# One-core two-block forward pass with a mixture of experts: the first two expert units' gates and ups put in a row, and down matrices loaded in two halves

## The chip, the cores and the metric

The program runs on one core of one Trainium2 chip. The metric is the device time of one execution in microseconds, from the first to the last work on the core. TensorE (PE) multiplies, VectorE (DVE) and ScalarE (ACT) work on tiles, GpSimd (POOL) issues the indirect DMAs, and SyncE (SP) issues nearly all weight loads, which 16 DMA engines carry.

## The reference

Float32 throughout, 512 tokens of width 1024. Block one: attention over a learned choice of keys, sliding-window attention, a dense MLP. Block two: gated linear attention and pooling, then the experts. Only the end of block two is touched:

```python
g_p, g_idx = lax.top_k(jax.nn.softmax(g_logits, axis=-1), 1)         # 1 of 4 groups
e_top, e_idx = lax.top_k(e_logits, TOP_K_IN_GROUP)                   # 2 of its 8 experts
gate = g_p * jax.nn.softmax(e_top, axis=-1)
def expert_block(args):                                              # D_EXPERT = 256
    xb, e = args
    return (jax.nn.silu(xb @ w_gate[e]) * (xb @ w_up[e])) @ w_down[e]
x = x + hier_moe(h2, ...)                                            # 32 experts, two per token
return rmsnorm_2(x, norm_f_g)
```

Gate, up and down of one expert are 1 MB each, so the experts need about 100 MB of weights.

## The kernel before, in words

The kernel runs five engines by hand with semaphores. Everything up to the residual stream of block two takes the first 1050 us and is not touched except for loads that start there. Then come 17 **units** (`UNITS_E`, q = 0 to 16). A unit is one or two experts of 64 rows each, stacked on 128 partitions; `places_of(q)` gives the numbers n of its experts' buffers in order of loading, `buffer_of(q)` the buffer of `xe` that holds its token rows.

Work of a unit, in the order of the data:

- POOL gathers its rows from `x_rows` in HBM into `xe` (line 691).
- PE turns them into `side` banks (`turn_rows_of`, line 2066), DVE copies them with the gain into `xeT` (`rows_turned`, line 1759).
- PE multiplies with gates and ups (`gate_up_part`, line 2408, 64 matmuls for two experts): the first 16 (`first_gates_of`, two parts of 8) run ahead, between the steps of the unit before, the other 48 in `gate_up_of`.
- ACT makes the silu (line 1159), DVE multiplies with the ups (`hidden`, line 1766), PE turns the result, ACT copies it, PE multiplies with the down matrices (`down_of`, line 2425, 16 matmuls).
- DVE adds to `xe` (`y_of`, line 1776). POOL scatters to `part_rows` (line 695). From unit 2 on (`FINISH_FROM`) the tokens that are then complete are normalised (`finish`, line 1787) and stored.

SP issues the loads in one order, each with a wait for the buffer's last reader: `gu` has 6 buffers (gates and ups of one expert, 2 MB, in four DMAs of 512 KB), `dn` has 8 (a down matrix, one DMA of 1 MB, `load_down`, line 548). SP's queue is in order: a wait holds back all loads behind it. Units 3 and 4 (`PIECED_E`) are loaded in quarters as units 0 and 1 release theirs (`gate_up_in_quarters`, line 613):

```python
for q in range(PIECED_E.start, EXTRA_AT + 1):
    for n in places_of(q):
        if n >= D_BUFS:
            sp.wait_ge(S("down_done"), unit_of(n - D_BUFS) + 1)
            down(n)
    if q in PIECED_E:
        gate_up_in_quarters(q)
        continue
```

Beside units 0 and 1, DVE also works out where the tokens go that an expert has beyond 64 rows: `late_columns` and `overflow_columns` (lines 1833 to 1864), `place_overflow` (1869 to 1881), `list_overflow` (1917 to 1921, after a small PE product, line 2478), and `name_late_experts` (1885 to 1908), whose last instruction raises `over_ready`. `gfin` is the final gain, broadcast to all partitions.

Of the kernel before, what the change touches and what calls it, by code (L numbers as in the profile page):

```python
# [13 lines left out]
P = 128  # L14
# [28 lines left out]
def buffer_of(q):  # L43

    return q if q < X_FIRST else (0, 1, 4, 5, 2, 3)[(q - X_FIRST) % X_BUFS]
# [202 lines left out]
def gated_blocks(nc, A, out):  # L248
# [8 lines left out]
    with stack:  # L257
# [107 lines left out]
        xe, _ = lay(b_at, ("xe", [P, X_BUFS, D]))  # L365
# [5 lines left out]
        assert temps_end <= b_at + 3 * half_buf  # L371
# [8 lines left out]
        below = place("below", [1, OVER, NE], b_at + words([P, X_FIRST + 1, D]))  # L380
        slotv = place("slotv", [P, 2, COLS], -(-tab_end // 64) * 64)
        gfin = place("gfin", [P, D], base + 4 * CONST_COLS["cos"][0])
# [67 lines left out]
        def _(sp):  # L450
# [151 lines left out]
            sp.dma_start(gfin[:, :], A["norm_f_g_2"].partition_broadcast(P)).then_inc(S("small_in"), 16)  # L602
# [62 lines left out]
        def _(pool):  # L665
# [24 lines left out]
            def gather(n, rows, done):  # L690
                pool.indirect_dma_start(xe[:, n, :], None, x_rows, bass.IndirectOffsetOnAxis(ap=rows, axis=0),
                                        bounds_check=row_bound, oob_is_err=False).then_inc(done, 16)

            def scatter(n, slots, done):
                pool.indirect_dma_start(part_rows, bass.IndirectOffsetOnAxis(ap=slots, axis=0), xe[:, n, :], None,
                                        bounds_check=row_bound, oob_is_err=False).then_inc(done, 16)

            def gather_parts(n, tokens, done):
                pool.indirect_dma_start(xe[:, n, :], None, part_rows, bass.IndirectOffsetOnAxis(ap=tokens, axis=0),
                                        bounds_check=row_bound, oob_is_err=False).then_inc(done, 16)  # L700

            def store_rows(n, tokens, done):
                pool.indirect_dma_start(out, bass.IndirectOffsetOnAxis(ap=tokens, axis=0), xe[:, n, :], None,
# [25 lines left out]
            for q in range(X_FIRST):  # L729
                gather(q, tabi[:, 1, q:q + 1], S(f"gathered{q}"))  # L730
            pool.wait_ge(S("slots_ready"), 1)
            pool.wait_ge(S("y_zeroed"), 16 * NT)
            for q in range(LAST_E):
# [7 lines left out]
                if q in (LAST_E - 3, LAST_E - 1):  # L741
                    pool.drain()
# [3 lines left out]
                if n < UNITS_E:  # L746
                    if q < 2:
                        scattered(q)
                    if q == 2:
                        pool.wait_ge(S("over_listed"), 1)  # L750
                        pool.wait_ge(S("over_ready"), 1)
# [5 lines left out]
                if q + 1 in MIXED_E:  # L757
                    scattered(q)
# [30 lines left out]
            for n in range(X_BUFS):  # L789
                pool.wait_ge(S(f"gathered{n}"), 16 * ((LAST_E - n) // X_BUFS + 1))  # L790
            store_unit(LAST_E)
# [35 lines left out]
        def _(act):  # L827
# [336 lines left out]
            def squares_of(q):  # L1164
# [3 lines left out]
                for n in range(2):  # L1168
                    act.wait_ge(*((S("y_made"), q + 1) if q < LAST_E else (S("last_y_made"), n + 1)))
                    chain(a(side[3][:, :], xe[:, buffer_of(q), n * L:(n + 1) * L], ACT.Square, accum_out=gw[:, 10 + n, one_]))  # L1170
# [15 lines left out]
            def overflow(i):  # L1186
# [3 lines left out]
                nc.scalar.copy(over_v[:, 0:1], slotv[:, 0, bass.ds(i + PAIRS, 1)]).then_inc(S("over_scale_set"), 1)  # L1190
                act.wait_ge(S("over_scale_set"), i)
# [6 lines left out]
                for n in range(2):  # L1198
                    a(side[3][:, :], xe[:, OVER_X, n * L:(n + 1) * L], ACT.Square, accum_out=gw[:, 10 + n, 1:2])\
                        .then_inc(S("over_guessed"), 1)  # L1200
                    act.wait_ge(S("over_guessed"), i * 5 + (n - 4))
                a(gw[:, 3, 1:2], gw[:, 10, 1:2], ACT.Identity, scale=1.0 / D, bias=eps_t[:, :]).then_inc(S("over_guessed"), 1)
                act.wait_ge(S("over_guessed"), i * 5 + (-2))
# [1365 lines left out]
```

## Time and profile before

| what | value |
|---|---|
| median of 3 runs | 1306.07 us (1304.95 to 1306.09) |
| the profiled execution's own time | 1303.1 us |
| its span, first to last instruction | 1301.1 us |
| mean granted TensorE clock | 0.992 |
| PE, DVE, ACT, POOL busy, of the span | 96%, 49%, 40%, 44% |
| expert units | from 1056 us to the end |
| last row store issued | 1298.07 us |

Times in the rows are microseconds from the span's start. The span is 2.0 us shorter than its execution, and that execution is 3.0 us under the median of the runs. PE's busy share is high, but it is a share of the whole program; what bounds the last 245 us has to be read from windows of that stage.

### The profile page before, as it was taken

What the parts mean: (1) busy time and instruction counts of PE and PEld (TensorE: products, weight loads), DVE (VectorE), ACT (ScalarE), POOL (GpSimd) and SP (SyncE); (2) the same over time, 40 slices, a digit from 0 to 9 for tenths busy, and PEclk for the clock granted to TensorE, in tenths of its full rate; (3) what the DMA queues carried; (4) which work ended last, traced back from release to release, by engine and by line L of the source; (5) the groups of instructions that cost most, each with busy time, mean ns of one, the idle gap of its engine ahead of it and who ended that gap; (6) DMA issues with size and microseconds to landing.
All of it is one profiled execution on the core that took longest, in us unless ns stands there. A gap on an engine that the chain in (4) does not pass through costs nothing.

```text
span 1301.1 us, 18979 instructions
## 1 busy us (share of the span) xinstructions
PE 1255.3 (96%) x6642; PEld 960.5 (74%) x6642; DVE 640.0 (49%) x1248; ACT 522.9 (40%) x884; POOL 568.9 (44%) x715
## 2 busy tenths in 40 slices
PE   7999999999999999999999999999999989998896
PEld 6767777787888888888888788777888865554462
DVE  4868768725542422222225765757243276342443
ACT  5657544435444324133144534145322300543444
POOL 4633323334655655555545664424644212341321
PEclk9999999999999999999999999999999999998899
DMA  6422222112334333333333333322427999999996
GB/s 219 109 65 55 67 58 65 50 49 81 98 96 113 115 97 97 115 97 113 97 98 97 97 96 83 82 49 70 126 81 265 359 331 386 417 417 416 417 417 246
DMA packets 223104, 208.38 MB, mean 160 GB/s; under 512 B 36034, under 2 KB 197556, under 8 KB 218804
## 3 DMA queue, kind: packets, MB, share of 16 engines
q1 hardware_dynamic: 209728, 191.87, 44.7%
q0 software_dynamic: 9504, 13.66, 2.8%
q10 hardware_dynamic: 3796, 1.86, 0.5%
q8 instruction: 45, 0.74, 0.2%
q14 instruction: 31, 0.25, 0.1%
HBM read 209.43 MB, written 20.45 MB: 177 GB/s over the span
## 4 chain that ended last, share of the span: by engine, by line
issue 40%; POOL 31%; PE 19%; DMA 4%; DVE 3%; SPq 2%; POOLq 1%; ACT 0%; DVEq 0%; ACTq 0%
POOL wlo L670 31%; PE bank L2408 4%; PE bank L2036 3%; PE bank L2038 3%; PE bank L2037 3%; PE bank L2425 3%; SPq L543 1%; DMA gu<-in_w_exp_up 1%; DMA xe<-part_rows,tabi 1%; PE side L2066 1%; DMA part_rows<-xe,tabi 1%; DMA xe<-x_rows,tabi 1%; PE side L2038 1%; PE side L2037 1%; PE side L2036 1%
## 5 line engine op out<-in xcount | busy, mean ns | idle before, releaser
L670 POOL TENSOR_TENSOR wlo<-raw,whi 128x256 fp32r<-128x256 f32 x644 | 497.6, 804 | 525.9 <-ACT whi L838 525.7
L2037 PE MATMUL bank<-actB_lo,whi 128*128 128x512 f32 x608 | 236.7, 389 | 0.0
L838 ACT ACTIVATE whi<-raw 128x1024 fp32r<-128x1024 f32 x161 | 169.0, 1051 | 152.6 <-PE bank L2038 125.0
L2036 PE MATMUL bank<-actB_hi,whi 128*128 128x512 f32 x576 | 227.8, 395 | 0.5 <-POOL wlo L670 0.5
L2038 PE MATMUL bank<-actB_hi,wlo 128*128 128x512 f32 x576 | 224.4, 390 | 0.0
L2036 PE MATMUL bank<-actA_hi,whi 128*128 128x512 f32 x400 | 157.0, 392 | 1.7 <-DVE actA_lo L1269 1.6
L2038 PE MATMUL bank<-actA_hi,wlo 128*128 128x512 f32 x400 | 155.7, 389 | 0.0
L2037 PE MATMUL bank<-actA_lo,whi 128*128 128x512 f32 x400 | 155.7, 389 | 0.0
L2408 PE MATMUL bank<-gu,xeT 128*64 128x256 f32 x1088 | 128.4, 386 | 8.5 <-issue 5.9
L2037 PEld LDWEIGHTS bank<-actB_lo,whi 128*128 128x128 f32 x608 | 114.2, 188 | 24.0 <-issue 1.0
L2036 PEld LDWEIGHTS bank<-actB_hi,whi 128*128 128x128 f32 x576 | 108.2, 188 | 25.9 <-issue 2.3
L2038 PEld LDWEIGHTS bank<-actB_hi,wlo 128*128 128x128 f32 x576 | 108.1, 188 | 22.8
L2408 PEld LDWEIGHTS bank<-gu,xeT 128*64 128x64 f32 x1088 | 80.6, 139 | 51.5 <-issue 19.3
L2059 PE MATMUL bank<-actA_hi,whi 128*128 128x512 f32 x216 | 95.0, 440 | 0.0
L2036 PEld LDWEIGHTS bank<-actA_hi,whi 128*128 128x128 f32 x400 | 75.1, 188 | 19.5 <-DVE actA_lo L1269 3.5
L2038 PEld LDWEIGHTS bank<-actA_hi,wlo 128*128 128x128 f32 x400 | 75.1, 188 | 15.8
L2037 PEld LDWEIGHTS bank<-actA_lo,whi 128*128 128x128 f32 x400 | 75.1, 188 | 15.3 <-issue 0.2
L1464 DVE TENSOR_SCALAR relu_u<-bank 128x512 f32<-128x512 f32 x32 | 22.1, 692 | 128.7 <-PE bank L2038 128.7
L2061 PE MATMUL bank<-actA_hi,wlo 128*128 128x512 f32 x216 | 85.0, 393 | 0.0
L2060 PE MATMUL bank<-actA_lo,whi 128*128 128x512 f32 x216 | 84.5, 391 | 0.0
L1478 DVE TENSOR_TENSOR ytmp<-bank,rs 128x512 f32<-128x512 f32 x32 | 22.1, 692 | 95.8 <-PE bank L2038 95.8
L2425 PE MATMUL bank<-dn,hidT 128*64 128x512 f32 x256 | 61.4, 624 | 2.7 <-ACT hidT L1162 2.7
(448 smaller groups left out, 1703.3 us busy)
## 6 DMA issues: line engine op xcount, KB each, us to landing
gu<-in_w_exp_gate SPq DMA_DIRECT2D x64, 512.0 KB, 15.4
gu<-in_w_exp_up SPq DMA_DIRECT2D x64, 512.0 KB, 16.3
dn<-in_w_exp_down SPq DMA_DIRECT2D x30, 1024.0 KB, 17.8
raw<-in_w_in SPq DMA_DIRECT2D x57, 512.0 KB, 3.8
raw<-in_w_up SPq DMA_DIRECT2D x32, 512.0 KB, 3.9
raw<-in_w_down SPq DMA_DIRECT2D x32, 512.0 KB, 3.7
raw<-in_w_out SPq DMA_DIRECT2D x16, 512.0 KB, 3.8
raw<-in_w_in SPq DMA_DIRECT2D x16, 256.0 KB, 3.2
```

The source lines that it names most:

```text
L670: ins = nc.gpsimd.tensor_tensor(wlo[:, slot, at], raw[:, slot, at], whi[:, slot, at].bitcast(F32), ALU.subtract)
L838: a(whi[:, c % RING, :], raw[:, c % RING, :], ACT.Copy).then_inc(hi_made, 1)
L1464: chain(v.tensor_scalar(relu_u[:, m % 2, :], out_bank(up + m)[:, :], 0.0, None, ALU.max), chunk_freed)
L1478: chain(v.tensor_tensor(ytmp[:, :], out_bank(c)[:, :], rs[:, :], ALU.mult), chunk_freed)
L2036: mm(b[:, :], w_hi, hi[:, k, :], start=first, stop=False)
L2037: mm(b[:, :], w_hi, lo[:, k, :], start=False, stop=False)
L2038: ins = mm(b[:, :], w_lo, hi[:, k, :], start=False, stop=last)
L2059: mm(b[:, :], w_hi, actA_hi[:, k, :], start=k == 0, stop=False)
L2060: mm(b[:, :], w_hi, actA_lo[:, k, :], start=False, stop=False)
L2061: ins = mm(b[:, :], w_lo, actA_hi[:, k, :], start=False, stop=k == NK - 1)
L2408: ins = mm(b[ROWS * h:ROWS * (h + 1), g * DE:(g + 1) * DE], xeT[:, j, k, ROWS * h:ROWS * (h + 1)], gu[n % GU_BUFS][:, g, k, :], start=k == ...
L2425: ins = mm(bank[2 + n][ROWS * h:ROWS * (h + 1), :], hidT[:, j, k * P + ROWS * h:k * P + ROWS * (h + 1)], w[:, k, n * L:(n + 1) * L], start ...
```

## The change

SP: a down matrix is loaded by two DMAs of 512 KB, one for each of its two blocks of 128 rows (k). Both units of `PIECED_E` are loaded before the down matrices of unit 4. The final gain is split in two halves of 512 columns: the first where constants were, the second on the place of `below`, the scratch tile of `name_late_experts`, so its load waits for `over_ready`. PE: gates and ups of units 0 and 1 run in a row, then the hidden rows and downs of unit 0; the table product of the overflow comes after unit 1's downs. DVE: its parts move along. POOL: five units' rows are gathered at the start, not four, since the sixth buffer (`xe_far`) lies apart; the buffers rotate in another order. The last unit is finished in halves by DVE and ACT (`finish_last`). In the overflow loop, which does not run with these inputs, semaphores are joined.

```diff
-    return q if q < X_FIRST else (0, 1, 4, 5, 2, 3)[(q - X_FIRST) % X_BUFS]
+    return q if q < X_FIRST else (5, 4, 0, 1, 2, 3)[(q - X_FIRST) % X_BUFS]
...
-        xe, _ = lay(b_at, ("xe", [P, X_BUFS, D]))
+        xe, gfin_at = lay(b_at, ("xe", [P, X_BUFS - 1, D]))
...
-        gfin = place("gfin", [P, D], base + 4 * CONST_COLS["cos"][0])
+        xe_far = place("xe_far", [P, D], base + 4 * CONST_COLS["cos"][0])
+        gfin = (place("gfin0", [P, L], base + 4 * CONST_COLS["before"][0]), place("gfin1", [P, L], gfin_at))
...
-                sp.dma_start(dn[n][:, :, :].rearrange("p (o j) n -> p o (j n)", o=1), wd_v[:, at_, :])\
-                  .then_inc(loaded, 16)
+                for k in range(2):
+                    sp.dma_start(dn[n][:, k:k + 1, :], wd_v[:, at_, k * D:(k + 1) * D]).then_inc(loaded, 16)
...
-            sp.dma_start(gfin[:, :], A["norm_f_g_2"].partition_broadcast(P)).then_inc(S("small_in"), 16)
+            sp.dma_start(gfin[0][:, :], A["norm_f_g_2"][0:L].partition_broadcast(P)).then_inc(S("small_in"), 16)
...
             for q in range(PIECED_E.start, EXTRA_AT + 1):
+                if q in PIECED_E:
+                    gate_up_in_quarters(q)
                 for n in places_of(q):
                     if n >= D_BUFS:
                         sp.wait_ge(S("down_done"), unit_of(n - D_BUFS) + 1)
                         down(n)
+                if q == PIECED_E.stop - 1:
+                    sp.wait_ge(S("over_ready"), 1)
+                    sp.dma_start(gfin[1][:, :], A["norm_f_g_2"][L:].partition_broadcast(P)).then_inc(S("small_in"), 16)
                 if q in PIECED_E:
-                    gate_up_in_quarters(q)
                     continue
...
-            for q in range(X_FIRST):
-                gather(q, tabi[:, 1, q:q + 1], S(f"gathered{q}"))
+            for q in range(X_FIRST + 1):
+                gather(buffer_of(q), tabi[:, 1, q:q + 1], S(f"gathered{q}"))
...
-                chain(v.scalar_tensor_tensor(xe[:, buffer_of(q), :], xe[:, buffer_of(q), :], gw[:, 13, one_], gfin[:, :],
-                                             ALU.mult, ALU.mult), S("rows_finished"))
+                for n in range(2):
+                    x = x_in(buffer_of(q))[:, n * L:(n + 1) * L]
+                    ins = v.scalar_tensor_tensor(x, x, gw[:, 13, one_], gfin[n][:, :], ALU.mult, ALU.mult)
+                chain(ins, S("rows_finished"))
+
+            def finish_last():
+
+                one_ = slice(LAST_E % NT, LAST_E % NT + 1)
+                first, second = (x_in(buffer_of(LAST_E))[:, n * L:(n + 1) * L] for n in range(2))
+                for n, x in enumerate((first, second)):
+                    dve.wait_ge(S("last_squared"), n + 1)
+                    chain(v.tensor_tensor(x, x, gfin[n][:, :], ALU.mult))
+                dve.wait_ge(S("guess_made"), guesses[0] + 1)
+                chain(v.tensor_tensor(gw[:, 12, one_], gw[:, 10, one_], gw[:, 11, one_], ALU.add))
+                refine(gw[:, 12, one_], gw[:, 13, one_], D, gw[:, 14, one_], gw[:, 15, one_], made=S("last_norm_made"))
+                chain(v.tensor_scalar(first, first, gw[:, 13, one_], None, ALU.mult), S("rows_finished"))
...
             turn_rows_of(0)
-            for q in range(LAST_E):
-                gate_up_of(q)
-                if q == 0:
-                    turn_rows_of(1)
-                elif q + 2 < UNITS_E:
+            gate_up_of(0)
+            turn_rows_of(1)
+            first_gates_of(1, 0)
+            first_gates_of(1, 1)
+            gate_up_of(1)
+            turn_hidden(0, 1)
+            turn_rows_of(2)
+            down_of(0)
+            for q in range(1, LAST_E):
+                if q > 1:
+                    gate_up_of(q)
+                if q + 2 < UNITS_E:
                     turn_rows_of(q + 2)
+                first_gates_of(q + 1, 0)
+                turn_hidden(q % 2, q + 1)
+                first_gates_of(q + 1, 1)
+                down_of(q)
```

SP's queue from the first quarter loads of unit 3 on (`dn_144` and `dn_145` belong to unit 4, `dn_146` and `dn_147` to unit 5). Before:

```order
L613 DMA gu_138<-in_w_exp_up 128x1024 [waits gate_up_done]
L613 DMA gu_139<-in_w_exp_up 128x1024
L548 DMA dn_144<-in_w_exp_down 128x2048 [waits down_done]
L548 DMA dn_145<-in_w_exp_down 128x2048 [waits down_done]
L613 DMA gu_140<-in_w_exp_gate 128x1024 [waits quarter_used]
```

The same queue in the changed kernel, from the last quarter of unit 4 on:

```order
L618 DMA gu_140<-in_w_exp_up 128x1024 [waits gate_up_done]
L618 DMA gu_141<-in_w_exp_up 128x1024
L554 DMA dn_144<-in_w_exp_down 128x1024 [waits down_done]
L554 DMA dn_144<-in_w_exp_down 128x1024
L554 DMA dn_145<-in_w_exp_down 128x1024 [waits down_done]
L554 DMA dn_145<-in_w_exp_down 128x1024
L631 DMA gfin_176<-in_norm_f_g 128x512 [waits over_ready]
L554 DMA dn_146<-in_w_exp_down 128x1024 [waits down_done]
```

The downs of unit 4 moved behind all eight quarter loads of unit 4, and between them and the downs of unit 5 there is now a load that waits for DVE's `over_ready`.

DVE's queue at the overflow lists of unit 1 (`xe` rows are `y_of(1)`, `below` begins `name_late_experts`). Before:

```order
L1766 SCALAR_TENSOR_TENSOR hid<-bank,slotv,hid 128x128x2 [waits silu_made,over_placed]
L1917 TENSOR_SCALAR prod<-side 128x9 [waits over_table_full]
...
L1759 TENSOR_TENSOR xeT<-side,small 128x512 [waits xe_used,over_listed]
L1759 TENSOR_TENSOR xeT<-side,small 128x512 [waits xe_used]
L1776 SCALAR_TENSOR_TENSOR xe<-bank,slotv,xe 128x512 [waits down_done]
L1776 SCALAR_TENSOR_TENSOR xe<-bank,slotv,xe 128x512
L1885 TENSOR_TENSOR below<-prod,con 1x512
```

After:

```order
L1771 TENSOR_TENSOR xeT<-side,small 128x512 [waits xe_used,over_placed]
L1771 TENSOR_TENSOR xeT<-side,small 128x512 [waits xe_used]
L1788 SCALAR_TENSOR_TENSOR xe<-bank,slotv,xe 128x512 [waits down_done]
L1788 SCALAR_TENSOR_TENSOR xe<-bank,slotv,xe 128x512
L1943 TENSOR_SCALAR prod<-side 128x9 [waits over_table_full]
...
L1911 TENSOR_TENSOR below<-prod,con 1x512 [waits over_listed]
```

The list now stands between `y_of(1)` and the naming of the late experts, and unit 1's hidden rows stand further ahead, before `y_of(0)`.

## Rows read from the trace of the kernel before

**Rows 1.** The page's 40 slices: what the DMA engines moved, GB/s.
```profile
GB/s 219 109 65 55 67 58 65 50 49 81 98 96 113 115 97 97 115 97 113 97 98 97 97 96 83 82 49 70 126 81 265 359 331 386 417 417 416 417 417 246
```

**Rows 2.** Windows of the expert stage; the last two numbers are DMA share and GB/s.
```profile
1060.00:1061.00 1.00, 1.00 (x14) 0.79 (x12) 0.86 (x5) 0.00 (x0) 0.00 (x0) 1.00 0.22 61
1061.00:1062.00 1.00, 1.00 (x12) 0.82 (x10) 0.83 (x6) 0.00 (x0) 0.00 (x0) 1.00 0.91 279
1060.00:1095.90 35.90, 33.60 (x283) 20.64 (x280) 28.51 (x95) 2.96 (x5) 4.21 (x4) 1.00 0.96 349
1060.00:1073.70 13.70, 12.50 (x95) 7.65 (x92) 10.96 (x41) 1.13 (x2) 0.00 (x0) 1.00 0.90 305
1135.00:1140.00 5.00, 5.00 (x34) 2.21 (x32) 1.41 (x3) 4.34 (x9) 1.02 (x1) 1.00 1.03 407
1165.00:1170.00 5.00, 3.97 (x36) 2.60 (x32) 2.45 (x5) 0.74 (x1) 3.04 (x3) 1.00 1.02 427
1095.00:1283.00 188.00, 170.07 (x1212) 95.82 (x1208) 68.89 (x147) 80.58 (x151) 58.39 (x54) 0.95 1.03 416
```

**Rows 3.** Timeline of the end: downs of unit 15, gates, ups, last finish.
```profile
1274.22 5.31 PE L2425 MATMUL bank<-dn,hidT 128*64 128x512 f32 x16 [0.68 <-ACT hidT L1162]
1279.36 3.63 PE L2408 MATMUL bank<-gu,xeT 128*64 128x256 f32 x32
1283.80 3.67 PE L2408 MATMUL bank<-gu,xeT 128*64 128x256 f32 x32 [0.81 <-DMA gu<-in_w_exp_up]
1295.98 1.28 DVE L1787 SCALAR_TENSOR_TENSOR xe<-xe,gw,gfin 128x1024 f32<-128x1024 f32 x1
```

**Rows 4.** Timeline of PE at units 0 to 2: start, busy, instructions.
```profile
1057.70 7.13 PE L2408 MATMUL bank<-gu,xeT 128*64 128x256 f32 x64 [0.51 <-DVE xeT L1759]
1067.10 1.08 PE L2408 MATMUL bank<-gu,xeT 128*64 128x256 f32 x8 [1.20 <-DVE xeT L1759]
1069.40 3.60 PE L2425 MATMUL bank<-dn,hidT 128*64 128x512 f32 x16
1072.93 1.15 PE L2066 MATMUL side<-con,xe 128*128 128x128 f32 x8
1080.70 1.17 PE L2478 MATMUL side<-placed,at_row 128*64 128x72 f32 x31 [0.21 <-DVE placed L1881]
1087.44 5.35 PE L2408 MATMUL bank<-gu,xeT 128*64 128x256 f32 x48
```

**Rows 5.** Timeline of DVE at units 0 and 1: first and last instruction of its parts.
```profile
1077.58 0.42 DVE L1869 TENSOR_TENSOR placed<-con,pos 128x264 f32<-128x264 f32 x1
1080.21 0.43 DVE L1881 TENSOR_TENSOR placed<-placed,vals 128x264 f32<-128x264 f32 x1
1081.99 0.17 DVE L1917 TENSOR_SCALAR prod<-side 128x9 f32<-128x9 f32 x1 [0.62 <-PE side L2478]
1083.82 0.18 DVE L1921 COPY slotv<-side 64x30 f32<-64x30 f32 x1
1087.66 1.41 DVE L1776 SCALAR_TENSOR_TENSOR xe<-bank,slotv,xe 128x512 f32<-128x512 f32 x2 [2.34 <-PE bank L2425]
1088.99 0.67 DVE L1885 TENSOR_TENSOR below<-prod,con 1x512 f32<-1x512 f32 x1
1093.50 0.14 DVE L1908 CAST over_n<-prod 1x1 int32<-1x1 f32 x1
```

**Rows 6.** Timeline of SP's queue: when loads are issued, and how long that takes.
```profile
1059.68 2.53 SPq L613 DMA_DIRECT2D gu<-in_w_exp_gate  x4
1073.04 0.94 SPq L548 DMA_DIRECT2D dn<-in_w_exp_down  x2
1087.66 0.80 SPq L548 DMA_DIRECT2D dn<-in_w_exp_down  x2
```

**Rows 7.** POOL's DMA queue (packets, MB, share), then from issue to landing of line 543's loads.
```profile
q0 software_dynamic: 9504, 13.66, 2.8%
...
DMA to landing us min/median/max: 3.9/16.3/25.2
```

More of the change, by code:

```diff
@@ L745, in _ @@
                 n = q + X_FIRST
[L746 to L749, printed above, removed]
+                if X_FIRST < n < UNITS_E:
+                    if q == 1:
                         pool.wait_ge(S("over_listed"), 1)
-                        pool.wait_ge(S("over_ready"), 1)
                     if q - 2 >= FINISH_FROM:
@@ L1169, in squares_of @@
                     act.wait_ge(*((S("y_made"), q + 1) if q < LAST_E else (S("last_y_made"), n + 1)))
-                    chain(a(side[3][:, :], xe[:, buffer_of(q), n * L:(n + 1) * L], ACT.Square, accum_out=gw[:, 10 + n, one_]))
+                    chain(a(side[3][:, :], x_in(buffer_of(q))[:, n * L:(n + 1) * L], ACT.Square, accum_out=gw[:, 10 + n, one_]),
+                          S("last_squared") if q == LAST_E else None)
                     if n == 0:
@@ L1212, in _ @@
             squares_of(LAST_E)
+            act.wait_ge(S("last_norm_made"), 1)
+            second = x_in(buffer_of(LAST_E))[:, L:]
+            a(second, second, ACT.Copy, scale=gw[:, 13, LAST_E % NT:LAST_E % NT + 1]).then_inc(S("last_squared"), 1)
         @block.vector
@@ L1986, in overflow @@
+                dve.wait_ge(S("over_dve_step"), i * 6 + (-1))
                 v.scalar_tensor_tensor(gw[:, 13, 1:2], gw[:, 15, 1:2], 1.5, gw[:, 13, 1:2], ALU.add, ALU.mult)\
-                    .then_inc(S("over_finished"), 1)
-                dve.wait_ge(S("over_finished"), i * 5)
+                    .then_inc(S("over_dve_step"), 1)
+                dve.wait_ge(S("over_dve_step"), i * 6)
                 dve.wait_ge(S("over_scattered"), i * 32 + (-16))
-                v.scalar_tensor_tensor(xe[:, OVER_X, :], xe[:, OVER_X, :], gw[:, 13, 1:2], gfin[:, :], ALU.mult, ALU.mult)\
-                    .then_inc(S("over_rows_done"), 1)
+                for n in range(2):
+                    x = x_in(OVER_X)[:, n * L:(n + 1) * L]
+                    ins = v.scalar_tensor_tensor(x, x, gw[:, 13, 1:2], gfin[n][:, :], ALU.mult, ALU.mult)
@@ L2005, in _ @@
                                        ALU.mult, ALU.add).then_inc(S("last_y_made"), 1)
-            finish(LAST_E)
+            finish_last()
         @block.tensor
@@ L2433, in down_landings @@
             def down_landings(n):
-                return 16 * len([m for m in range(n % D_BUFS, n + 1, D_BUFS) if m != SPARE])
+                return sum(16 if m >= places_of(LAST_E)[0] else 32 for m in range(n % D_BUFS, n + 1, D_BUFS) if m != SPARE)
             def down_of(q):
@@ L2467, in _ @@
             turn_rows_of(0)
[L2468 to L2472 removed]
+            gate_up_of(0)
[6 more added lines that the diff above has]
+            down_of(0)
+            for q in range(1, LAST_E):
+                if q > 1:
+                    gate_up_of(q)
+                if q + 2 < UNITS_E:
                     turn_rows_of(q + 2)
+                first_gates_of(q + 1, 0)
+                turn_hidden(q % 2, q + 1)
+                first_gates_of(q + 1, 1)
+                down_of(q)
                 if q == 1:
```

103 lines of the change are left out of this document (50 added, 53 removed).

## The prediction

> **What bounds the kernel now.** The page's slices come first: what the DMA engines move rises from about 100 GB/s to 417 GB/s in the last ninth of the span and stays there [rows 1]. So the stage of the experts is read by windows. From 1095 to 1283 us the DMA engines move 416 GB/s at a share of 1.03 [rows 2]: they are full for 188 us. The reader should see next that this isn't so before: from 1060 to 1095.9 us they average 349, because in 1060 to 1061 they move 61 and then climb slowly. Then the end. PE has its last gates at 1279.36 and waits before the last ups for their DMA, 0.81 us, until 1283.80 [rows 3]; what follows is one chain without slack to 1301.1. So the end hangs on when the last ups land, and that on how many bytes had been moved before the engines became full. But the wait is only 0.81 us: PE itself is nearly as late. A later load stream moves the end one for one; an earlier one gives back 0.8 us, unless PE is earlier too.
>
> The currency is therefore: bytes moved by about 1095 us, at 416 GB/s.
>
> **Gates and ups in a row (PE, DVE).** Before, unit 0's 64 matmuls run from 1057.70 for 7.13 us, unit 1's first 8 at 1067.10, unit 0's downs (3.60 us) at 1069.40, to 1073.0 [rows 4]. After, PE turns unit 1's rows (1.15 us) from 1064.8, and DVE copies them ahead of unit 0's hidden rows, so unit 1's gates can begin at about 1066.2. 64 matmuls of 7.13 us end at 1073.4. Then hidden rows (about 0.4) and rows of unit 2 (1.15): 1075.0. Unit 0's downs: 1078.6, 5.6 us later than before. Rows of unit 3 (1.15), and the 16 first gates of unit 2 with unit 1's hidden rows between them (1067.10 to 1069.40 before, 2.3): 1082.1. Unit 1's downs: 1085.8. The table product (1.17): 1087.0. Unit 2's other 48 matmuls start there, against 1087.44 before [rows 4]. PE comes out of the rearrangement where it was.
>
> Releases for SP move: the eight quarter loads of unit 4 are issued from 1068.1 to 1073.4 or so, behind those of unit 3. Before, they stood behind unit 0's downs and went out from about 1074 on; the downs of unit 4 were issued at 1073.04 [rows 6]. Now these follow at 1078.6. So the hole before 1075 is filled.
>
> **The wait for over_ready (SP).** It stands in SP's queue ahead of the downs and of gates and ups of unit 5 and of all later ones. When is it raised? DVE: y of unit 0 from 1078.7 (1.4 us); then the placing, which took from 1077.58 to 1080.64, 3.1 us [rows 5]: 1083.2; rows of unit 3 (1.3): 1084.5; y of unit 1 (1.41) after its downs: 1087.3; the list, 1081.99 to 1084.00 before, 2.0: 1089.3; the naming, 1088.99 to 1093.64 before, 4.65 [rows 5]: **1094.0**. In the kernel before it was raised at 1093.64, and SP had no need of it there. It had issued the downs of unit 5 at 1087.66 [rows 6].
>
> Flow starts some 1.5 us behind an issue (issued 1059.68, 61 GB/s in the microsecond from 1060, 279 in the next [rows 2, 6]). So from 1095.5 on the stream runs again. When does it run dry? Unit 3's 4.19 MB take as long as before, to 1073.7 (305 GB/s over 13.7 us [rows 2]). Behind them stand unit 4's gates and ups, 4.19 MB, its two downs, 2.10 MB, and a scatter of POOL (13.66 MB over 66 transfers, 3 of them a whole matrix, leave about 0.17 MB each [rows 7]): 6.5 MB at 416 GB/s are 15.5 us, so dry at 1089.2. The engines have nearly nothing to do for 6.3 us.
>
> Against before: from 1060 to 1095.9 it moved 349 GB/s by 35.9 us, 12.5 MB [rows 2]; less four transfers of POOL (0.7), and less 0.4 us, 11.7 MB of weights by 1095.5. After: 4.19 + 4.19 + 2.10 = 10.5 MB. Missing 1.2 MB, 2.9 us. The second half of the gain (0.26 MB by its shape, 0.6 us) formerly went out in a gap; now it stands in the full stream, and I take 0.5. Sum **+3.4 us**. The restart: before, the first microseconds after the gap at 1060 ran near 300 GB/s, not 416 [rows 2]. Bounds: 0 (all engines full at once) and 2.0 us (seven microseconds at 300). The stream now restarts with downs and several loads at once, unlike the single pairs at 1060; I take **+0.7**.
>
> **Downs in halves.** 20 down matrices are issued whole in the full stretch (n = 10 to 17 and 19 to 30), 21 MB, 50 us of it. No row separates the rate of an 8 KB piece from one of 4 KB. Lower bound 0: gates and ups, in the 4 KB pieces, make two thirds of a stream that runs at 416. Upper bound: windows of 5 us lie between 407 and 427 GB/s [rows 2]; if all of this 4.8% were the piece's size, 50 us would grow by 2.4. I take **+1.0**, under the middle. For the downs loaded before 1095 it costs nothing, since a gap of the engines stands behind them; without that gap up to 10 more would cost 0.5. The Trainium skill speaks against this edit: "DMA: Bandwidth & Descriptors", section "Bandwidth", says to batch DMAs to 1 MiB or more. The trace agrees only for a DMA by itself (next part); in the full stream, of which four DMAs in five are already 512 KB, it still moves 416 GB/s. By that section's rule halving would cost much, by the row at most the 2.4.
>
> **The finish of the last unit.** Now the scaling of 1024 columns, 1.28 us from 1295.98, stands alone at the end [rows 3]. After, both halves are multiplied with the gain while ACT squares and takes the root; the second product (about 0.7) ends some 0.2 us after the root is ready, then the same five small steps, then one half on DVE beside one on ACT, about 0.65. -1.28 + 0.65 + 0.2: **-0.4 us**. No more than -0.6, and if the halves cost a handshake, 0.
>
> **Gather of unit 4 at the start.** It is off SP's queue and small. It takes away a short wait of PE at unit 4, and PE's lead grows by 1 or 2 us; that has no worth while loads bind.
>
> **Sum.** 3.4 + 0.7 + 1.0 - 0.4 = +4.7 us. On the profiled execution's span of 1301.1 that is 1305.8, on its own time of 1303.1 it is 1307.8; that execution lies 3.0 under the median of the runs, so against 1306.07 the forecast is 1310.8 us. A difference of 0.2% (2.6 us) is about what can be told from no change here.
>
> **Rivals.**
>
> 1. *The stream doesn't run dry, so the row of gates pays.* If over_ready comes before 1089, or the backlog reaches to it, the new order has by 1095.5 moved 4.2 + 21.8 x 0.416 = 13.3 MB, less 0.5 of POOL, 12.8 against 11.7 before: -2.6 us. With +1.0 for the halves, +0.5 for the gain and -0.4, -1.5; with halves for nothing -2.5; and PE, which has only 0.8 us to give, must have gained its own lead at unit 4. Time 1303.0 to 1304.5; I price it at 1303.3. For it: the gap at 1060 is real and is filled. Against: the DVE chain up to over_ready is long, in order and timed by rows 5. It decides at over_ready at 1091. Chance 0.2.
> 2. *A shorter gap.* Before had moved the same 10.5 MB by 1092.6. Each microsecond that over_ready comes earlier than 1094.0 gives one back; at 1091.5 with a cheap restart the whole is +1.5, 1307.6. For it: the list needs only PE's product, which might be done at once. Against: nothing in DVE's queue can overtake. Chance 0.19.
> 3. *PE falls to its lower clock at the end.* If gates and then ups of the last unit land late, PE stands idle between them; after such idleness the 16 downs of unit 15 took 5.31 us, where those at full clock take 3.60 [rows 3, 4]. Ups and downs at the low level would add up to 3.6 + 1.7. With one of them slow: 1310.8 + 2.7 = 1313.5. Chance 0.1.
> 4. *Each extra DMA pays its own start.* A lone 512 KB load takes at least 3.9 us to land [rows 7], but 1.26 us at 416 GB/s: 2.6 us of fixed time. Were that not overlapped, 20 more DMAs would cost 53 us, 1364. This is what that rule of the skill's page amounts to here. Against: 112 loads of that size already run without it. Chance 0.01.
>
> The forecast itself has 0.5. Its own range is 1308.0 to 1314.0 (restart 0 to 2, halves 0 to 2.4, over_ready up to 1 us off). The range for 8 in 10 reaches down into the first rival and up over the third: 1303.2 to 1314.5. Slower by over 0.2%: forecast, third and fourth, 0.61; within 0.2%: 0.21 (the second, and the upper part of the first); faster by over 0.2% (under 1303.5): 0.18.
>
> **What the profile after would show.** Right: SP issues the quarters of unit 4 before 1074 and then, between the downs of unit 4 (1078 to 1080) and the half of the gain, nothing until about 1094; windows of 1090 to 1095 are nearly empty; the 416 GB/s start at 1096 and end some 4 or 5 us later than before; the last ups land near 1288; PE waits there for more than the 0.81 us of before. Wrong: over_ready before 1091; no window near 1092 under 300 GB/s; a mean rate in the full stretch of 413 or less (then the halves cost more than 1 us) or still 416 (then nothing); PE late rather than the loads, with no wait for the last ups, which would mean that the arithmetic in bytes is the wrong currency.

## The result: 1.0% slower, more than double what was forecast

The changed kernel takes 1317.71 us (median of 4 runs, 1317.03 to 1320.72) where the kernel before took 1305.51 beside it. The ratio is 1.0102, 95% interval 1.0081 to 1.0123: 13.3 us more, between 10.6 and 16.1. The forecast was + 4.7 us; the direction was right, the size was not, and the time lies outside the range of 1308.0 to 1314.0 and also outside the wider one of 1303.2 to 1314.5. The profiled execution took 1318.26 us, its span is 1316.2.

The load stream first. The page's slices of the changed kernel answer to [rows 1]: GB/s moved, and above it PE's granted clock in tenths.

```profile
PEclk9999999999999999999999999999999999998898
...
GB/s 225 100 64 65 65 49 64 50 64 80 96 110 98 115 93 119 100 88 126 88 97 100 86 96 97 64 50 81 126 61 393 354 341 332 412 418 416 414 414 122
```

Windows of the same kernel, as in [rows 2]; the last three numbers are the granted clock, the DMA share and GB/s.

```profile
1085.00:1090.00 5.00, 5.00 (x66) 4.11 (x64) 3.72 (x14) 0.00 (x0) 0.09 (x1) 1.00 0.92 370
1090.00:1095.00 5.00, 4.53 (x39) 3.34 (x35) 4.45 (x18) 0.74 (x1) 3.26 (x3) 1.00 0.36 93
1095.00:1100.00 5.00, 4.93 (x29) 2.15 (x31) 1.13 (x4) 0.38 (x1) 0.99 (x1) 1.00 0.88 261
1105.00:1283.00 178.00, 150.68 (x1040) 84.79 (x1040) 62.55 (x141) 70.94 (x132) 48.34 (x48) 0.93 1.03 415
...
1295.00:1300.00 5.00, 5.00 (x46) 3.73 (x44) 3.60 (x10) 3.85 (x10) 1.17 (x2) 1.00 0.01 0
```

The hole is where the prediction put it: from 1090 to 1095 the engines move 93 GB/s, from 1095 to 1100 they come back to 261, and from 1105 to 1283 they move 415. Its cause shows on DVE, the last naming instruction, and in SP's queue: downs of unit 4, half of the gain, downs of unit 5 (answers to [rows 5, 6]).

```profile
1094.17 0.14 DVE L1934 CAST over_n<-prod 1x1 int32<-1x1 f32 x1
```

```profile
1079.36 1.75 SPq L554 DMA_DIRECT2D dn<-in_w_exp_down  x4
1094.34 0.33 SPq L631 DMA_DIRECT2D gfin<-in_norm_f_g  x1
1094.71 2.22 SPq L554 DMA_DIRECT2D dn<-in_w_exp_down  x4
```

So far this is the forecast. The end is not. PE's timeline of the end, which answers to [rows 3]:

```profile
1290.43 5.35 PE L2454 MATMUL bank<-dn,hidT 128*64 128x512 f32 x16 [0.68 <-ACT hidT L1170]
1295.59 7.11 PE L2437 MATMUL bank<-gu,xeT 128*64 128x256 f32 x64
...
1304.36 3.65 PE L2560 MATMUL bank<-dn,hidT 128*64 128x512 f32 x16 [0.47 <-ACT hidT L1170]
```

PE doesn't wait for the last ups any more: all 64 gates and ups of the last unit run in one piece from 1295.59, while the DMA engines move nothing at all (the window above). The loads are done; it is PE that is late. The chain that ended last, followed through the stage, names where. Columns are start, duration and what it was:

```profile
1132.09 17.67 DMA gu<-in_w_exp_gate
1157.82 6.08 PE bank L2437 x48
1178.59 8.82 issue
1188.13 6.44 DMA xe<-part_rows,tabi
1200.58 7.53 issue
1208.83 6.44 DMA xe<-part_rows,tabi
1222.44 5.28 PE bank L2454 x16
```

The reader should see two fetches of partial rows (`part_rows`), one for each of the two mixed units, 8 and 9, each behind 7 to 9 us of "issue", time in which the engine waited for nothing that the profile shows. POOL issues these fetches. Its timeline has the same pair:

```profile
1174.88 1.01 POOL L704 DMA_INDIRECT part_rows<-xe,tabi  x1 [7.75 <-DVE xe L1788]
...
1188.13 1.02 POOL L708 DMA_INDIRECT xe<-part_rows,tabi  x1 [9.54 <-issue]
1196.87 1.01 POOL L704 DMA_INDIRECT part_rows<-xe,tabi  x1 [7.72 <-DVE xe L1788]
...
1208.83 1.02 POOL L708 DMA_INDIRECT xe<-part_rows,tabi  x1 [8.25 <-issue]
```

Between the scatter of unit 8 (1196.87) and the fetch for unit 9 (1208.83) lie 11.96 us. In the kernel before they were 7.1, as its own timeline of POOL shows. Its first two rows are the scatter of unit 7 and the fetch for unit 8: there 12.2 us lay between the two without any drain, since the scatter landed only at 1176.87, behind the loads of the spare expert that POOL had issued from 1156.79 to 1159.41 and the last of which landed at 1174.82. The changed kernel has 13.3 us there, so at unit 8 it is not far from the kernel before; what the drain costs at that place shows only against experiment 3. The last row is that of the old drain, at the third unit from the end:

```profile
1164.97 1.03 POOL L695 DMA_INDIRECT part_rows<-xe,tabi  x1 [4.57 <-DVE xe L1776]
...
1177.13 1.02 POOL L699 DMA_INDIRECT xe<-part_rows,tabi  x1 [8.48 <-DMA part_rows<-xe,tabi]
1187.21 1.02 POOL L695 DMA_INDIRECT part_rows<-xe,tabi  x1 [9.05 <-DVE xe L1776]
...
1194.30 1.02 POOL L699 DMA_INDIRECT xe<-part_rows,tabi  x1 [3.43 <-DMA part_rows<-xe,tabi]
...
1257.78 1.02 POOL L695 DMA_INDIRECT part_rows<-xe,tabi  x1 [9.55 <-issue]
```

What the change put between them is one line, `pool.drain()`, ahead of the fetch at both mixed units; the drain that stood three units from the end went. Neither the description of the change nor the lines of the diff shown with it have this; it stands only in the whole diff. PE pays for it through DVE, whose y of unit 9 waits for the parts, with unit 10's hidden rows behind it in DVE's queue. DVE, then PE:

```profile
1215.36 1.41 DVE L1788 SCALAR_TENSOR_TENSOR xe<-bank,slotv,xe 128x512 f32<-128x512 f32 x2 [14.26 <-DMA xe<-part_rows,tabi]
```

```profile
1200.04 0.69 PE L2095 MATMUL side<-con,hid 128*128 128x128 f32 x2 [6.09 <-DVE hid L1778]
...
1219.85 0.69 PE L2095 MATMUL side<-con,hid 128*128 128x128 f32 x2 [4.98 <-DVE hid L1778]
```

### The profile page after: what moved, and what is told of

Read it like the earlier page. It is cut to its first block, busy times and chain, and to the rows that moved or that the text cites. A ratio compares the mean times of both kernels' runs of the same rounds, so it can differ in the third digit from the quotient of the medians.

```text
span 1316.2 us, 19043 instructions
## 1 busy us (share of the span) xinstructions
PE 1260.0 (96%) x6642; PEld 965.8 (73%) x6642; DVE 637.3 (48%) x1264; ACT 523.2 (40%) x885; POOL 566.7 (43%) x715
## 4 chain that ended last, share of the span: by engine, by line
issue 43%; POOL 35%; PE 13%; DMA 3%; DVE 3%; SPq 1%; POOLq 1%; ACT 1%; another core or an unknown queue 0%; ACTq 0%; DVEq 0%
POOL wlo L679 35%; PE bank L2437 6%; PE bank L2454 4%; DMA gu<-in_w_exp_gate 1%; DMA xe<-part_rows,tabi 1%; PE side L2095 1%; DMA raw<-in_w_out 1%; SPq L554 1%; DVE hid L1778 0%; SPq L548 0%; ACT hid L1167 0%; DVE xe L1788 0%; PE bank L2560 0%; POOLq L676 0%
## 5 line engine op out<-in xcount | busy, mean ns | idle before, releaser
L2437 PEld LDWEIGHTS bank<-gu,xeT 128*64 128x64 f32 x1088 | 84.6, 139 | 49.3 <-issue 14.5
L2454 PE MATMUL bank<-dn,hidT 128*64 128x512 f32 x256 | 64.9, 653 | 4.8 <-ACT hidT L1170 4.1
```

What stands on the lines that cost most here:

```text
L2437: ins = mm(b[ROWS * h:ROWS * (h + 1), g * DE:(g + 1) * DE], xeT[:, j, k, ROWS * h:ROWS * (h + 1)], gu[n % GU_BUFS][:, g, k, :], start=k == ...
L2454: ins = mm(bank[2 + n][ROWS * h:ROWS * (h + 1), :], hidT[:, j, k * P + ROWS * h:k * P + ROWS * (h + 1)], w[:, k, n * L:(n + 1) * L], start ...
```

## Theories

- **A, the hole starves PE.** The nearly 2 MB that are missing by 1105 make PE wait at units 6 and 7 (1.6 and 5.2 us for gates), it falls to its low clock, and is late for good.
- **B, the drains.** POOL's drains at units 8 and 9 lengthen a chain that PE follows; loads have no part in it. The hole then adds its own bytes and no more.
- **C, the halves.** DMAs of 512 KB in place of 1 MB cost the stream more than was seen.

All times of a kernel below stand beside runs of the kernel before on the same chip, median 1303.8 to 1303.9 us.

## Experiments

**1. The wait later in SP's queue (e1_gain_later).** The changed kernel, with this moved from ahead of the downs of unit 5 to behind its gates and ups:

```diff
             for q in range(PIECED_E.start, EXTRA_AT + 1):
...
-                if q == PIECED_E.stop - 1:
-                    sp.wait_ge(S("over_ready"), 1)
-                    sp.dma_start(gfin[1][:, :], A["norm_f_g_2"][L:].partition_broadcast(P)).then_inc(S("small_in"), 16)
...
                     gate_up(n)
+                if q == PIECED_E.stop:
+                    sp.wait_ge(S("over_ready"), 1)
+                    sp.dma_start(gfin[1][:, :], A["norm_f_g_2"][L:].partition_broadcast(P)).then_inc(S("small_in"), 16)
```

> The changed kernel, with the wait for over_ready and the second half of the gain moved in SP's queue from ahead of the downs of unit 5 to behind the gates and ups of unit 5. Theory A (the missing 2 MB make PE wait at units 6 and 7, it drops to its low clock, and is then late for good): DMA moves over 300 GB/s from 1090 to 1095 where it moved 93, PE's waits of 1.6 and 5.2 us for gates at 1131 and 1145 go, unit 7's gates start near 1150.5 and not at 1157.65, and the time falls by 7 us or more, to 1304 to 1310. Theory B (POOL's drains at the two mixed units make PE late there, whatever was loaded): the waits at units 6 and 7 go, but those before units 9 and 10 grow as before, and the time falls by no more than 4 us, to 1314 or more. Theory C (halved downs): no more than the 4 us of the hole come back, 1313.7.

Measured: 1313.63 us, ratio 1.0081 (1.0064 to 1.0098), + 10.6 us. Some 3 us come back, not 7. All queues together have moved 44.01 MB by 1105 where the changed kernel had moved 41.38 (packets that start between 980 and 1105 us), so the hole is gone; the drains are not. PE at unit 7, and POOL at unit 9:

```profile
1147.24 1.95 PE L2437 MATMUL bank<-gu,xeT 128*64 128x256 f32 x8 [4.82 <-DMA gu<-in_w_exp_gate]
```

```profile
1193.08 1.00 POOL L704 DMA_INDIRECT part_rows<-xe,tabi  x1 [7.58 <-DVE xe L1788]
...
1204.91 1.02 POOL L708 DMA_INDIRECT xe<-part_rows,tabi  x1 [8.14 <-issue]
```

Theory A fails its test of the time. It also fails one of place: PE's wait at unit 7 is still there, 4.82 us, without the hole (more on it at the end). Theory B had the time within 0.4 us, but said that this wait would go. Theory C had named the same time, 1313.7; the next experiment is the one that tells B from C.

**2. Whole downs in the changed kernel (e2_whole_downs).** `load_down` issues one DMA per matrix again, and PE counts 16 landings for it.

> The changed kernel, with each down matrix loaded by one DMA of 1 MB again. Theory A: the hole stays, so the time stays within 2 us of 1317.7, and DMA moves 416 to 417 GB/s from 1110 to 1280 in place of 415. Theory B: the same, within 2 us. Theory C (512 KB pieces cost the stream and the landing of each down): 4 us or more come back, 1313.7 or less.

Measured: 1318.86 us, ratio 1.0110 (1.0093 to 1.0126). Nothing comes back; theory C falls as the cause of the 13. The rate of 416 to 417 that all theories expected was missed: the window from 1110 to 1280 has 411. A PE that is late also frees buffers late, which would explain it; no run here separates that. Where PE binds, the stream can't show what a piece's size costs.

**3. Drains as before (e3_drains_as_before).**

```diff
-                if q == LAST_E - 1:
+                if q in (LAST_E - 3, LAST_E - 1):
                     pool.drain()
...
                 if q + 1 in MIXED_E:
-                    pool.drain()
                     scattered(q)
                     parts_of_unit(q + 1)
```

> The changed kernel, with POOL's drains where they stood before (none at the mixed units, one at the third unit from the end, one at the last). Theory B: parts of unit 9 are asked for some 7 us behind the scatter of unit 8 and not 12, PE's 5 us wait before unit 10 goes, and 3 to 8 us come back: 1309.7 to 1314.7. Theory A: PE is already 10 us late when it comes to unit 8, the end moves by the 3 us of unit 10 at most, 1314.7 to 1317.7. Theory C: no change, 1317.7.

Measured: 1308.04 us, ratio 1.0032 (1.0022 to 1.0042). Nine of the 13 us come back with nothing but the drains moved. (That their old place costs nothing is experiment 11.) POOL's scatters of units 7 and 8 and the fetches behind them:

```profile
1174.21 1.01 POOL L704 DMA_INDIRECT part_rows<-xe,tabi  x1 [7.61 <-DVE xe L1787]
...
1182.58 1.02 POOL L708 DMA_INDIRECT xe<-part_rows,tabi  x1 [4.65 <-DMA part_rows<-xe,tabi]
1191.56 1.00 POOL L704 DMA_INDIRECT part_rows<-xe,tabi  x1 [7.96 <-DVE xe L1787]
...
1198.17 1.02 POOL L708 DMA_INDIRECT xe<-part_rows,tabi  x1 [2.90 <-DMA part_rows<-xe,tabi]
```

8.4 and 6.6 us from scatter to fetch, where the changed kernel had 13.3 and 12.0: each drain cost POOL 5 us. And the end is again one in which PE waits for loads, as in [rows 3]:

```profile
1287.29 3.67 PE L2436 MATMUL bank<-gu,xeT 128*64 128x256 f32 x32 [1.32 <-DMA gu<-in_w_exp_up]
```

The hole is in this kernel, and it is 4.2 us slower than before (2.9 to 5.5). The prediction's + 4.7, which was for everything but the drains, lies in that interval.

**4. Only the wait, in the kernel before (e4_before_wait).** `sp.wait_ge(S("over_ready"), 1)` ahead of the downs of unit 5.

> The kernel before, with one wait for over_ready added in SP's queue ahead of the downs of unit 5, and nothing else. over_ready was raised at 1093.64 there, SP had issued those downs at 1087.66: 6 us of SP's queue, of which the backlog hides some. Theory A: by 1095 the engines have moved 1.5 to 2.5 MB less, PE waits at unit 6 or 7, and the time rises by more than the missing bytes at 416 GB/s: 1306.07 + 6 to 12, 1312 to 1318. The rule of my prediction (a later stream moves the end one for one): + 3.6 to 6, 1309.7 to 1312. Theory B or C alone: within 2 us of 1306.07.

Measured: 1305.71 us, ratio 1.0018 (1.0008 to 1.0027), + 2.3 us (1.0 to 3.5): under both expectations that saw a cost. SP issued the downs of unit 5 at 1092.91 and not at 1087.66, yet the trace has only 1.02 MB less by 1120 and 0.98 MB less by 1280: 2.4 us at 416 GB/s. The rest of the 5 us was covered by loads already issued. PE did wait at unit 7, 5.08 us (its 48 matmuls start at 1154.74, not 1150.46), and the end is later by no more than the missing bytes. So bytes are the right currency for a change in the loads, and theory A's step from a wait of PE at unit 7 to a late end doesn't hold.

**5. Only the halves, in the kernel before (e5_before_halves).** `load_down` as in the changed kernel.

> The kernel before, with each down matrix loaded by two DMAs of 512 KB, and nothing else. My term for this was + 1.0 us (bounds 0 and 2.4). The profile of the changed kernel moved 415.1 GB/s from 1110 to 1280 us where that of before moved 416.5, 0.6 us over the 188 us of the full stretch. Theory A and theory B (POOL's drains): + 0.6 to 1.0 us, the last ups land no more than 1 us later than 1284.2. Theory C (the halves cost the stream or one of its 16 engines more): + 2.4 us or more.

Measured: 1305.21 us, ratio 1.0011 (1.0002 to 1.0020): + 1.4 us (0.3 to 2.6), between what theories A and B (0.6 to 1.0) and theory C (2.4 or more) had said. By 1280 it has moved 0.46 MB less, 1.1 us. The last ups start at 1285.07 where they started at 1283.80 before.

**6. Experiments 1 and 3 together (e6_later_drains).**

> The changed kernel, with both edits together: the wait for over_ready and the second half of the gain behind the gates and ups of unit 5, and POOL's drains where they stood before. The first alone gave 1313.63 us, the second alone 1308.04, where before had 1303.88. If the two causes each set the end when the other is gone (the load stream by its missing 2 MB, POOL by its drains), then both together come to what is left of the change: halves, second gain in the stream, finish, which I sum to + 0.6 + 0.5 - 0.4: 1303.9 + 0.7 = 1304.6, range 1302.5 to 1306.5. If instead PE's wait at unit 7 is what makes it late, the time stays at 1307 or more, since the wait stayed in the first run.

Measured: 1303.98 us, ratio 1.0002 (0.9994 to 1.0011). No hole, no drains, no difference from before. Against experiment 3 the hole is worth 4 us; against experiment 1 the drains are worth about 10. The window of the hole, and the full stretch:

```profile
1090.00:1095.00 5.00, 4.46 (x37) 2.98 (x35) 4.51 (x17) 1.12 (x2) 2.16 (x3) 1.00 1.03 413
...
1105.00:1283.00 178.00, 157.71 (x1126) 88.05 (x1126) 68.13 (x155) 80.80 (x151) 52.14 (x52) 0.96 1.03 412
```

**7. And whole downs (e7_all_three).**

> As the kernel with both edits (e6_later_drains), and down matrices whole again. Against that kernel this undoes the halves alone, where nothing but loads bind: theory A and B, 0.6 to 1.0 us less. Theory C: 2.4 us less or more. It should also show whether the row of gates by itself gains anything over before: by my first rival, up to 2.6 us less than 1303.9.

Measured: 1302.17 us, ratio 0.9986 (0.9977 to 0.9994): 1.8 us faster than before (0.8 to 3.0), the only version here that is, though by less than 0.2%, and experiment 11 doesn't repeat it. Against experiment 6, run beside it, the halves cost 1.8 us, more than theories A and B had said (0.6 to 1.0) and less than theory C (2.4). With experiment 5, the halves cost 1.4 to 1.8 us here. What is left of the change, the row of gates above all, has 0.65 MB more moved by 1280, 1.6 us. Its full stretch and its last wait:

```profile
1105.00:1283.00 178.00, 159.58 (x1134) 90.87 (x1134) 68.17 (x155) 80.14 (x150) 51.23 (x51) 0.95 1.03 414
```

```profile
1282.71 3.67 PE L2436 MATMUL bank<-gu,xeT 128*64 128x256 f32 x32 [0.74 <-DMA gu<-in_w_exp_up]
```

**8. Only the drains, in the kernel before (e8_before_drains).** `pool.drain()` ahead of `scattered(q)` at the mixed units.

> The kernel before, with a drain of POOL ahead of each mixed unit's parts (units 8 and 9) as in the changed kernel, and nothing else: the load stream is untouched. Theory B: the parts are asked for 5 us later at each (in the changed kernel 12.0 us after the scatter of unit 8, in the one with drains as before 6.6), PE comes 8 to 10 us later to unit 11 than 1214.25, PE ends behind the loads, and the time rises by 4 to 9 us. Theory A (drains only matter once PE has been made late by loads): within 2 us of before.

Measured: 1310.71 us, ratio 1.0055 (1.0039 to 1.0072): + 7.2 us (5.1 to 9.4), with the stream nearly untouched (115.89 MB by 1280, before 116.10). POOL at unit 9, 13.1 us from scatter to fetch; then PE's last unit, in one piece with no wait for its ups, as in the changed kernel:

```profile
1192.46 1.02 POOL L695 DMA_INDIRECT part_rows<-xe,tabi  x1 [8.45 <-DVE xe L1777]
...
1205.56 1.02 POOL L699 DMA_INDIRECT xe<-part_rows,tabi  x1 [9.41 <-issue]
```

```profile
1287.58 7.11 PE L2409 MATMUL bank<-gu,xeT 128*64 128x256 f32 x64
```

PE starts the 48 matmuls of unit 11 at 1224.18, 9.9 us later than before. Theory B holds alone, with nothing else changed.

**9. What the drain waits for (e9_landings_for_drains).** The changed kernel, with this in place of each of the two drains:

```diff
                 if q + 1 in MIXED_E:
-                    pool.drain()
+                    pool.wait_ge(S(f"gathered{n % X_BUFS}"), 16 * (n // X_BUFS + 1))
+                    pool.wait_ge(S("rows_stored"), 16 * (q - FINISH_FROM))
```

> The changed kernel, where POOL at each of the two mixed units waits for the landing of the gather and of the store that it issued last, in place of the drain. If the drain costs what it waits for, the landings of POOL's own transfers (the two are issued up to 2.7 us behind the scatter and land some 4 to 5 us later), the parts of unit 9 are asked for some 8 us behind the scatter of unit 8, against 12.0 with the drain and 6.6 with nothing, and 5 to 8 us of the 9 that the drains cost come back: 1309.5 to 1313. If the landings account for all of it, no change, 1317. If the drain's cost is all its own, as without drains, 1308.

Measured: 1314.98 us, ratio 1.0095 (1.0079 to 1.0111), + 12.4 us, where the drains make it + 13.3 and neither (experiment 3) + 4.2. The expected 8 us from scatter to fetch were wrong; it is 11.8:

```profile
1194.99 1.00 POOL L704 DMA_INDIRECT part_rows<-xe,tabi  x1 [7.97 <-DVE xe L1789]
...
1206.82 1.02 POOL L708 DMA_INDIRECT xe<-part_rows,tabi  x1 [8.12 <-DMA out<-xe,tabi]
```

The store of finished rows, issued 2.7 us behind the scatter, lands 8 us after its issue in this full stream, not the 4 to 5 that I had assumed. At unit 9 that alone makes up the drain's time (11.8 against 12.0); at unit 8 it is 11.9 us against 13.3. So the drain costs about what it costs to wait for these two landings, transfers of POOL that the fetch doesn't need. Whether it waits for just these isn't settled by equal lengths; the 1.4 us at unit 8 are open.

**10. One drain (e10_one_drain).** The changed kernel without that of unit 9; that of unit 8 stays.

> The changed kernel without the drain ahead of unit 9's parts; that ahead of unit 8's stays. Each drain costs POOL about 5 us, in a chain that runs scatter, parts, y, scatter through both units. If they add up, half of the 9 us comes back: 1312.5 to 1313.5. If the first is covered by PE's wait for the spare expert at unit 9 (5.94 us before), nearly all comes back: 1308 to 1310.

Measured: 1308.58 us, ratio 1.0040 (1.0025 to 1.0056), nearly the time of experiment 3, which has neither. POOL and PE:

```profile
1188.17 1.02 POOL L708 DMA_INDIRECT xe<-part_rows,tabi  x1 [9.77 <-issue]
1196.84 1.00 POOL L704 DMA_INDIRECT part_rows<-xe,tabi  x1 [7.65 <-DVE xe L1789]
...
1203.36 1.02 POOL L708 DMA_INDIRECT xe<-part_rows,tabi  x1 [2.83 <-DMA part_rows<-xe,tabi]
```

```profile
1207.35 5.35 PE L2438 MATMUL bank<-gu,xeT 128*64 128x256 f32 x48
...
1284.76 7.11 PE L2438 MATMUL bank<-gu,xeT 128*64 128x256 f32 x64
```

The time is as the second branch said, its reason is not. PE's wait for the spare expert didn't cover the first drain: unit 10's 48 matmuls start at 1207.35, 7.5 us later than in experiment 3 (1199.84). What makes it up comes later, in experiment 3: against this kernel it loses some 1.6 us at unit 10's hidden rows (a wait of 2.34), 3.1 us at the downs of units 12 and 15, which run at the lower clock there (5.35 and 5.08 us, here 3.65), and 1.7 us to waits for the loads of the last units. Its last ups start at 1287.29, when their load has landed. This kernel, late by a drain, is ready for them about a microsecond later than that and no longer waits. One drain uses up PE's slack against the loads; behind it nothing covers the second. In the changed kernel unit 11 starts at 1227.55, here at 1220.31, 7.2 us, and two sets of downs at the low clock (5.35 us each at 1248.98 and 1290.43, where this kernel has 3.65) make 3.4 more: 10.6 of the 10.8 us between the two spans. Put the other way, the second drain makes the fetch for unit 9 5.5 us later (1208.83, here 1203.36), and the downs of units 10, 12 and 15, at the lower clock behind it, add 5.2.

**11. Without the other drain (e11_fewer_drains).** Experiment 7 without the drain at the third unit from the end.

> The fastest version so far (e7_all_three, 1302.17 against 1303.87 of before: gain behind unit 5, whole downs, drains as before), without the drain three units from the end, so that POOL drains once, at the last unit but one. That drain kept POOL 9.51 us in the profile of the version. Its scatter is waited for by nobody at once: if PE's loads bind there, no change, 1302.2 within 1 us; if POOL's lateness reached the end, up to 2 us less.

Measured: 1303.23 us, ratio 0.9996 (0.9987 to 1.0005); against the kernel before of its own set 0.5 us faster, where experiment 7 was 1.8; the two intervals overlap. POOL now goes on to its scatter when the rows are there:

```profile
1254.53 1.01 POOL L704 DMA_INDIRECT part_rows<-xe,tabi  x1 [4.44 <-DVE xe L1787]
```

Nothing comes back. Where the drain stood before the change, it cost nothing that can be told here.

## Why the prediction was wrong

One step failed. The sum 3.4 + 0.7 + 1.0 - 0.4 has no term for POOL's drains: the prediction priced what the change does to the loads, to DVE's chain up to `over_ready` and to the finish, and passed over the drains that the change moved to units 8 and 9. They were worth 9 us in the changed kernel (experiment 3) and 7.2 alone (experiment 8).

What the engines moved in all queues since 980 us (packets by their start, counted from each trace from the span's start), against the times measured. "By bytes" is the difference by 1280 at 416 GB/s; the last two columns are us against before:

```
                     MB by 1120   by 1280   by bytes   measured
before                    49.49    116.10
changed kernel            47.62    114.02       +5.0      +13.3
gain later (1)            50.01    116.36       -0.6      +10.6
drains as before (3)      48.00    114.38       +4.1       +4.2
wait alone (4)            48.47    115.12       +2.4       +2.3
halves alone (5)          49.31    115.64       +1.1       +1.4
drains alone (8)          49.22    115.89       +0.5       +7.2
no hole, no drains (6)    50.37    116.71       -1.5       +0.3
and whole downs (7)       50.10    116.74       -1.6       -1.8
```

Four of the five experiments without the new drains follow their bytes within half a microsecond. Experiment 6 doesn't by its median, though its profiled execution was its fastest, 1301.77 us. The three kernels with both new drains don't follow them at all.

**What bounds the kernel: right for before, not carried over.** "A later load stream moves the end one for one" holds as long as PE isn't later. The text saw that PE is nearly as late, and then priced only what the change does to loads. So the list of parts was short by one: the move of POOL's drain stands in the change and got no term. Its price could have been bounded from the kernel before: the old drain shows there as an idle stretch of POOL of 9.55 us ahead of the scatter at 1257.78, and at unit 9 the fetch came 7.1 us behind the scatter, with PE idle 4.11 us for the hidden rows behind it. My own list of signs had the outcome, "PE late rather than the loads, with no wait for the last ups", as something that would mean that bytes are the wrong currency. They are the right one for loads. It was another engine's chain that became the bound.

**Rearranged units (right).** Unit 2's 48 matmuls run from 1086.97, as forecast (1087.0). SP's issues were forecast for 1068 to 1074 (quarters of unit 4) and 1078.6 (its downs); they came at 1069.33 to 1075.3 and 1079.36. The gather of unit 4 at the start did what was said too: PE comes to that unit's 48 matmuls at 1111.87, before at 1114.20.

**over_ready (right).** Forecast 1094.0; the instruction that raises it ends at 1094.31. Hole, restart and gain were + 4.1 us, net of what the row of gates moves earlier; the trace has 1.87 MB missing by 1120, 4.5 us, in the changed kernel, and 1.50 MB, 3.6 us, in experiment 3. The 4 us between experiments 3 and 6 aren't that term: they are the hole against a stream that already runs ahead of the one before, and so they hold the gain of the row of gates as well.

**Halves (a size, inside its bounds).** + 1.0 forecast; + 1.4 alone (0.3 to 2.6), + 1.8 between experiments 6 and 7. The Trainium skill's page "DMA: Bandwidth & Descriptors", section "Bandwidth", would batch to 1 MiB or more. The runs agree in sign. In size they speak against taking it as a fixed time for each DMA, which my fourth rival priced at 53 us: with the queue full it is 1 to 2 us for 20 more.

**The last finish (a size).** - 0.4 forecast. From the start of the last downs to the end of the span the changed kernel takes 1316.2 - 1304.36 = 11.8 us; before, 1301.1 - 1289.15 = 12.0. It gives 0.1 to 0.2. The scaling itself did shrink, from 1.28 us [rows 3] to a half on DVE, 0.48 us, and a half on ACT that starts at 1311.48, takes 0.72 and ends last. DVE's half:

```profile
1311.42 0.48 DVE L1814 TENSOR_SCALAR xe_far<-xe_far,gw 128x512 f32<-128x512 f32 x1
```

**Sum.** The forecast's terms made 4.7; the kernel that has all of them and not the new drains measures 4.2. The missing term is 9 us. That 4.7 and 4.2 lie so close is in part luck: the halves were priced 0.4 to 0.8 us too low and the finish gave 0.2 to 0.3 less than forecast, so what is left of the 4.2 for hole, restart and gain is some 2.5 to 3 us by the medians, not 4.1; each of these has an interval of 1 us or more to either side. Of the rivals, the third (the lower clock) took part, but not through late loads at the end: the downs of unit 15 ran at it before as well, and what came on top are those of units 9 and 12 (5.16 and 5.35 us, before 3.60 and 3.65). The first rival's premise, no hole, is experiment 6: priced at 1303.3, 2.8 us under the median of before, measured 0.3 over it (- 0.8 to 1.4). The halves (1.8, not 1.0) and the finish are 1 us of these 3.1; the rest isn't found, since the bytes of its profiled execution do show the gain.

## What to carry over

List every line of the diff with the engine it stands on before pricing any, waits and drains too: an instruction that moves no data can be the largest term. Here a drain cost POOL about as much as waiting for the landings of the gather and the store that it had issued last, 5 us each in a full stream; three units from the end, where nobody waits for POOL's next step, it cost nothing. When a stream of loads binds with PE close behind, price both chains: PE's slack took up one drain, and the second went to the end in full. A price that one experiment confirms (4.7 against 4.2) can still be made of terms that are off in opposite directions.

## What was not expected of the hardware

- Indirect transfers of POOL are slow to land in the full stream, and stores no less than scatters. From 1100 to 1290 in the kernel before, the scatters to `part_rows` landed 7.2 us (median; 5.6 to 11.9) behind their issue, the row stores 8.4 us (6.0 to 12.4). The 11.9 is the scatter of unit 7, behind the loads of the spare expert.
- PE waited 4.82 us for unit 7's gates in experiment 1 though no less had been moved by then (58.24 MB by 1140, before 57.78). Three things bear on it. PE was ready for them at 1142.42, and before, where it didn't wait, it came to them at 1144.73. SP had issued these loads at 1122.59 and 1127.50, before at 1119.59 and 1123.91: ahead of them stand the four halves of two down matrices, whose issue took 7.63 us from 1114.91 (two whole ones took 2.86). In experiment 5, with the halves alone, the issue is as late (1122.56) and PE waits 2.37 us. And the last landings were late: the trace records 45 of the 64 partial landings of these four loads, all but three by 1140.8, the others at 1142.8, 1145.5 and 1147.2; before, all 64 are there and the last is at 1144.2. Experiment 6 does the same up to the first mixed unit, has the gates at 1144.30 and waits 2.91 us, so the 2.9 us between the two may be nothing but one execution against another. Why the last shares were late in this one isn't known.
- PE's waits at the mixed units cost more than their length. Behind the one of 6.09 us in the changed kernel the 16 downs took 5.16 us, behind one of 4.11 us in the kernel before 5.52, where those at full clock take 3.60 [rows 4]: the granted clock was 0.50 there (windows of 1202.5 to 1205.5 and 1209 to 1212.5), its lower level of 1.2 GHz. The downs of units 12 and 15 in the changed kernel did the same (5.35 us) behind waits of only 1.35 and 1.55 us for the hidden rows. In experiment 10 waits of 1.23 and 1.55 us at the same places left them at 3.65 us and a clock of 1.00. What decides between the two isn't shown by any run here.
